# The ends of two attentions on TensorE: output products cut into parts, and the orders at the two layer borders changed

## What is computed

```
for l in range(2):
    proj = h @ w_in[l]            # a, g, zc, q, k, v, za, qi, ki, wi
    y_conv = silu(layer_norm(conv31(a * sigmoid(g)))) * silu(zc)
    y_attn = topk_masked_attention(q, k, v, qi, ki, wi) * silu(za)
    h = layer_norm(ALPHA * h + concat(y_conv, y_attn) @ w_out[l])
x = h[16:528]
z = rmsnorm(x) @ w_in_2           # q, k, v, gate_a, u, v_in, gate_b, g_merge
attn = softmax(q k^T) v * silu(gate_a)
gm = gelu(u) * mix(layernorm(gelu(v_in))) * silu(gate_b)
x = x + (g0 * (attn @ w_proj_attn) + g1 * (gm @ w_proj_gmlp)) @ w_out_2
out = rmsnorm(x)
```

## Time and profile before

| | |
|---|---|
| median of 3 runs | 1014.51 us (1014.0 to 1015.2) |
| the profiled execution | 1014.03 us, span 1012.2 us |
| mean granted clock of TensorE | 0.991 |
| TensorE busy | 982.5 us (97%) |
| VectorE busy | 668.4 us (66%) |
| ScalarE busy | 559.6 us (55%) |
| GpSimd busy | 232.4 us (23%) |
| chain that ended last | TensorE 80%, VectorE 10%, ScalarE 3%, DMA 2% |

### The profile page before, as it was taken

One profiled execution on the slowest core, in us unless ns is written; L12 is line 12 of the kernel. 1 busy time (PEld: TensorE's weight loads), 2 busy tenths in 40 slices (PEclk: granted clock), 3 DMA queues, 4 the chain that ended last, 5 costly groups with the idle time before them and its releaser, 6 DMA issues.

```text
span 1012.2 us, 15815 instructions
## 1 busy us (share of the span) xinstructions
PE 982.5 (97%) x6084; PEld 819.3 (81%) x6084; DVE 668.4 (66%) x1444; ACT 559.6 (55%) x920; POOL 232.4 (23%) x254
## 2 busy tenths in 40 slices
PE   8999999999999999999999999999999999999997
PEld 7888998986677988888878677888888788888886
DVE  4899999988673499999988756638522333333432
ACT  6685891655343568598165424544646566564442
POOL 0110671125212401077111511624101000000001
PEclk9999999999999999999999899999999999999999
DMA  8876885752001577487475300478777536366662
GB/s 299 198 183 169 214 195 135 174 118 85 1 1 66 143 186 175 121 192 183 125 170 122 118 21 1 169 172 199 180 215 198 116 87 162 88 162 129 173 160 83
DMA packets 23962, 143.92 MB, mean 142 GB/s; under 512 B 2880, under 2 KB 3648, under 8 KB 8272
## 3 DMA queue, kind: packets, MB, share of 16 engines
q0 software_dynamic: 8496, 60.36, 32.2%
q1 hardware_dynamic: 15392, 82.55, 23.0%
HBM read 140.81 MB, written 2.10 MB: 141 GB/s over the span
## 4 chain that ended last, share of the span: by engine, by line
PE 80%; DVE 10%; ACT 3%; issue 2%; POOL 2%; DMA 2%; SPq 1%; POOLq 0%; DVEq 0%; ACTq 0%
PE psum_B L1404 20%; PE psum_A L1404 13%; PE psum_B L1438 8%; PE psum_A L1438 8%; PE psum_A L1600 6%; DVE conv_acc L1918 4%; PE psum_C L1480 2%; PE psum_C L1404 2%; PE psum_A L1815 2%; PE psum_B L1815 2%; DMA w_raw<-in_weights 2%; PE psum_B L1544 2%; POOL w_lo L1184 2%; PE psum_B L1802 2%; PE psum_A L1516 2%
## 5 line engine op out<-in xcount | busy, mean ns | idle before, releaser
L1191 POOL DMA_DIRECT2D w_lo<-in_weights x59 | 52.0, 881 | 545.9 <-ACT w_lo L728 493.7
L1918 DVE SCALAR_TENSOR_TENSOR conv_acc<-u,vec,conv_acc 128x528 f32<-128x528 f32 (+1 forms) x240 | 172.4, 756 | 3.2
L1404 PE MATMUL psum_B<-x_hi,w_hi 128*128 128x272 f32 (+3 forms) x456 | 138.1, 337 | 0.5 <-ACT shifted L785 0.3
L1404 PE MATMUL psum_B<-x_hi,w_lo 128*128 128x272 f32 (+3 forms) x456 | 135.4, 331 | 0.0
L1404 PE MATMUL psum_B<-x_lo,w_hi 128*128 128x272 f32 (+3 forms) x456 | 135.3, 331 | 0.0
L727 ACT ACTIVATE w_hi<-w_raw 128x2048 fp32r<-128x2048 f32 (+2 forms) x73 | 113.4, 1553 | 25.8 <-DMA w_raw<-in_weights 25.3
L728 ACT ACTIVATE w_lo<-w_raw 128x2048 fp32r<-128x2048 f32 (+2 forms) x73 | 112.7, 1545 | 0.0
L1404 PE MATMUL psum_A<-x_hi,w_hi 128*128 128x272 f32 (+3 forms) x368 | 100.1, 315 | 0.8 <-DMA w_lo<-in_weights 0.4
L1404 PE MATMUL psum_A<-x_lo,w_hi 128*128 128x272 f32 (+3 forms) x368 | 98.1, 309 | 0.0
L1404 PE MATMUL psum_A<-x_hi,w_lo 128*128 128x272 f32 (+3 forms) x368 | 97.9, 309 | 0.0
L1404 PEld LDWEIGHTS psum_B<-x_hi,w_hi 128*128 128x128 f32 (+1 forms) x456 | 79.0, 187 | 10.0 <-issue 1.7
(11 more groups left out here) (409 smaller groups left out, 2294.9 us busy)
## 6 DMA issues: line engine op xcount, KB each, us to landing
w_raw<-in_weights SPq DMA_DIRECT2D x65, 1024.0 KB, 5.0
w_lo<-in_weights POOLq DMA_DIRECT2D x57, 1024.0 KB, 8.3
x_first<-in_x_t SPq DMA_DIRECT2D x8, 264.0 KB, 6.3
h<-in_x SPq DMA_DIRECT2D x1, 2048.0 KB, 9.8
out<-h SPq DMA_DIRECT2D x4, 512.0 KB, 2.6
w_raw<-in_weights SPq DMA_DIRECT2D x2, 512.0 KB, 7.6
post_ln_g<-in_post_ln_g SPq DMA_DIRECT2D x2, 512.0 KB, 4.6
post_ln_b<-in_post_ln_b SPq DMA_DIRECT2D x2, 512.0 KB, 6.3
```

What stands on the lines that cost most here:

```text
L1191: pool.dma_start(wlo[n % RING][:, 0:width], io["weights"][n, :, 0:width], accum_op=ALU.add) \
L1404: mm = pe.matmul(ps[0:cols, i, o:o + b - a], w[wp][:, kt, at:at + cols], x[xp][:, kt, a:b], start=(kt == 0 and wp + xp == 0), stop=(kt == ...
L1918: got = dve.scalar_tensor_tensor(dst, src, w, dst, ALU.mult, ALU.add)
```

## The change

The tables that hang work on the items change. In the first layer the last product of tile 3 (half 1) is cut in two: the convolution's part of tile 4 runs behind item 36, tile 3's first part behind item 37 and its second behind item 38, in bank 1 of `psum_C`. In the second layer the two parts of tile 3 stand behind items 28 and 29, and the convolution's part of tile 4 is cut into six products behind item 30 and six behind item 31. In the first layer the normalisation of tile 3 moves behind the loop, tile 3 is turned behind both attention parts, and the second half of GpSimd's second subtraction waits for tile 4's normalisation. Behind the second layer both `h_normed` buffers lie in `k`, the first two are written ahead of the gated output, ScalarE takes `x_hi` of tile 1 ahead of the weights, and `kv` of t = 3 stands two query products later, with tile 4 turned behind the first query product.

```
-        (34, 0, 3, "A"), (36, 1, 3, "A")),
-    1: ((17, 0, 1, "A"), (19, 0, 2, "B"), (21, 1, 1, "A"), (23, 1, 2, "A"), (26, 0, 3, "A"), (28, 1, 3, "A")),
+        (34, 0, 3, "A")),
+    1: ((17, 0, 1, "A"), (19, 0, 2, "B"), (21, 1, 1, "A"), (23, 1, 2, "A"), (26, 0, 3, "A")),
...
-OUTPUT_CONV_AT = {0: 38, 1: 30}
+LAST_OUTPUT_AT = {
+    0: ((36, "wo conv", 0, 0, 4), (37, "wo part", 0, 1, 3, "C", 0, 4), (38, "wo part", 1, 1, 3, "C", 0, 4)),
+    1: ((28, "wo part", 0, 1, 3, "A", 0, 4), (29, "wo part", 1, 1, 3, "A", 0, 4), (30, "wo conv", 0, 0, 2),
+        (31, "wo conv", 0, 2, 4)),
+}
...
-KV_AND_Q = (("kv", 0), ("kv", 1), ("kv", 2), ("q", 0, 0), ("kv", 3), ("q", 1, 0), ("q", 2, 0), ("q", 3, 0),
+KV_AND_Q = (("kv", 0), ("kv", 1), ("kv", 2), ("q", 0, 0), ("q", 1, 0), ("q", 2, 0), ("kv", 3), ("q", 3, 0),
...
-        hn = [sb("h_normed0", [P, D], at=K_AT + 4 * D), sb("h_normed1", [P, D], at=where[0])]
+        hn = [sb(f"h_normed{i}", [P, D], at=K_AT + 4 * D * i) for i in range(2)]
...
                 y_hi(l, "attn", 4)
+                if l == DEPTH - 1:
+                    x_hi(l, 1)
                 split_hi(after)
...
-                subtract_hi(after + 1)
-                ln_deviation((l, "post", 4), 4, P)
+                if l < DEPTH - 1:
+                    subtract_hi(after + 1, (0,))
+                    ln_deviation((l, "post", 4), 4, P)
+                    pool.wait_ge(normed.sem, normed.at((l, "x", 4)))
+                    subtract_hi(after + 1, (1,))
...
-                    if t == 2:
-                        turn_rows(1, 4)
                 else:
                     query_half(t, *half)
+                    if (t, *half) == (0, 0):
+                        turn_rows(1, 4)
```

More of the change, by code:

```diff
@@ L346, in attention_extras @@
         todo["dve"][i + 1].append(("residual", part, t))
+    todo["dve"][39 if l == 0 else 29].append(("residual", 1, 3))
     for t, i in POST_AT[l]:
@@ L353, in attention_extras @@
             todo["pool"][i + 1].append(("input", t))
-    todo["pe"][OUTPUT_CONV_AT[l]].append(("wo conv", 0))
+    for i, *op in LAST_OUTPUT_AT[l]:
+        todo["pe"][i].append(tuple(op))
+    if l == 0:
+        todo["dve"][39].append(("aggregate", 3))
+        todo["pool"][39].append(("deviation", "post", 3))
     if l == 0:
@@ L1585, in turn_rows, with output_half @@
                 mm.then_inc(psum_full.mark(use), 1)
-            def output_half(l, n, half, t, ps):
+            def output_half(l, n, half, t, ps, kks=range(4)):
                 part = ("conv", "attn")[half]
@@ L1593, in output_half @@
                     pe.wait_ge(meta_paired.sem, meta_paired.at((l, part)))
-                for kk in range(4):
+                for kk in kks:
                     kt = half * 4 + kk
@@ L1608, in output_rows, with output_part, output_conv @@
                 output_half(l, n, 1, t, ps).then_inc(psum_full.mark(use), 1)
-            def output_conv(l, n):
+            def output_part(l, half, n, t, buf, first, last):
+                use = (l, "wo", n, t)
+                ps = (bank[buf][:, 1:2, :] if half else claim(use, buf, (1,)))[:, 0, :]
+                mm = output_half(l, n, half, t, ps, range(first, last))
+                if half and last == 4:
+                    mm.then_inc(psum_full.mark(use), 1)
+            def output_conv(l, n, first=0, last=4):
                 buf, at = OUTPUT_BANK[n]
-                ps = claim((l, "wo", n, 4), buf, (at,))[:, 0, :]
-                output_half(l, n, 0, 4, ps).then_inc(psum_full.mark((l, "wo", n, 4, "conv")), 1)
+                ps = (bank[buf][:, at:at + 1, :] if first else claim((l, "wo", n, 4), buf, (at,)))[:, 0, :]
+                mm = output_half(l, n, 0, 4, ps, range(first, last))
+                if last == 4:
+                    mm.then_inc(psum_full.mark((l, "wo", n, 4, "conv")), 1)
             def output_attn(l, n):
@@ L1707, in woven @@
                             output_rows(l, *op[1:])
+                        elif op[0] == "wo part":
+                            output_part(l, *op[1:])
                         else:
@@ L1733, in _ @@
                     turn_rows(l, 2)
+                    output_attn(l, 1)
                 turn_rows(l, 3)
-                output_attn(l, 1)
+                if l == DEPTH - 1:
+                    output_attn(l, 1)
             SPARE = "B", (1,)
@@ L2125, in aggregate, with post_norm @@
                     .then_inc(stats_made.mark((l, "post", t)), 1)
-            def post_norm(l, t):
+            def post_norm(l, t, between=None):
                 n = SIZE[t]
@@ L2135, in post_norm @@
                     .then_inc(dve_step.mark((l, "gain", t)), 1)
+                if between:
+                    between()
                 dve.wait_ge(dve_step.sem, dve_step.at((l, "gain", t)))
@@ L2237, in _ @@
                     woven(i + 1)
-                y_part(l, "attn", 4)
                 if l < DEPTH - 1:
+                    post_norm(l, 3, lambda: y_part(l, "attn", 4))
                     x_lo(l, 0)
                     x_lo(l, 1)
+                    residual(l, 0, 4)
+                    x_lo(l, 2)
+                    residual(l, 1, 4)
+                    aggregate(l, 4)
+                    post_norm(l, 4)
+                    x_lo(l, 3)
                 else:
@@ L2245, in _ @@
                     second_input(2)
+                    y_part(l, "attn", 4)
+                    second_input(3)
                     x_lo(l, 1)
-                    second_input(3)
                     x_lo(l, 2)
[L2249 to L2256, removed]
+                    residual(l, 0, 4)
+                    x_lo(l, 3)
+                    residual(l, 1, 4)
+                    aggregate(l, 4)
+                    post_norm(l, 4)
                     second_input(4)
```

6 lines of the change are left out of this document (4 added, 2 removed).

## The result

The changed kernel takes 1017.64 us (median of 20 runs) where the kernel before takes 1013.73 (20 runs): a ratio of 1.0034, 95% interval 1.0023 to 1.0044, so 2.3 to 4.5 us slower. Two of the changed kernel's runs took 1199 and 1363 us at granted clocks of 0.75 and 0.66, and one of the kernel before 1082; the ratio leaves these three out (without them the medians are 1017.5 and 1013.6). The forecast was 1018.0 in a range of 1013.0 to 1021.5, and slower by over 0.2% with a chance of 0.60.

The account below looks back on a forecast made before the run. TensorE, busy 97% of the span, bounds the kernel. Minus 1.2 (first layer), plus 2.95 (late `vin` half 1), plus 1.7 (clock) is plus 3.45 on 1014.03: 1017.5, with 0.5 for the median 1018.0 us, range 1013.0 to 1021.5.

Parts of the forecast that it names:

- The step that decided: First product with `vin` half 1: the block lands at 691.6, TensorE stands 5.6 us, and the product starts 2.95 us later.
- Rival A: At `vin` half 1: the block arrives in time and the change does what it removes, 1010.6 us; chance 0.14.
- rival B: At `vin` half 1: TensorE stands, but at the short end of both transfers, 1015.9 us; chance 0.13.
- The chain: From `kv` of t = 3 to `vin` half 1: issue 0.2, load 8.1, copies and issue 4.1, adding DMA 9.6 us.
- The guess that the loads of `u` slow the adding DMA: At `vin` half 1: two `u` loads follow its adding DMA, taken at 9.6 us, bounds 8.1 and 10.8.
- The second layer's gain: Second layer's tail and border up to the queries: four waits of 3.10 us go, two cuts cost 0.4, minus 2.7 us.
- rival D: First query product: held up to 0.9 us by the copy of `kv` of t = 0; slower still, 1022.0 us; chance 0.10.
- The first layer's gain: First layer's tail: waits of 0.82 and 0.69 us go, 0.2 and 0.1 are added, minus 1.2 us.
- The 0.1 us for the second half of the last subtraction: First layer: GpSimd's second subtraction half starts only when tile 4 is normalised; product g may wait, 0.1 us taken.
- The clock: Behind the stand at `vin` half 1: TensorE's clock falls and costs 1.7 us, bounds 0 and 3.3.
- Rival C: At `vin` half 1: TensorE stands 5.6 us and the clock holds, 1016.3 us; chance 0.08.
- the forecast's sentence that two loads cost more than one: Adding DMA of `vin` half 1: two loads behind it cost it more than one does; no run showed two.

Follow-up runs that it names:

- experiment 1: Changed kernel, but `kv` of t = 3 stands one query product later than in the kernel before, not two: 1013.99 us, ratio 1.000.
- experiment 2: Kernel before with only the change's order of `kv` and `q` and tile 4 turned behind the first query product: 1022.52 us, ratio 1.0086.
- experiment 3: Changed kernel with `kv` of t = 3 and the turn of tile 4 at the places of the kernel before: 1011.84 us, ratio 0.998.
- experiment 7: Changed kernel, but GpSimd makes the low part of `vin` half 1 by subtractions, not an adding DMA: 1012.23 us, ratio 0.9979.
- experiment 6: Changed kernel, but the loads of both `u` blocks are issued only when the first `vin` product has ended: 1024.3 us, one run.
- experiment 4: Changed kernel with all edits to the second layer's end and the border behind it undone, only the first layer's part left: 1011.89 us, ratio 0.9979.
- experiment 5: Changed kernel with 24 products whose result nothing reads, between half 0 and half 1 of the first `vin` product: 1015.58 us, ratio 1.0014.
- second trace: Changed kernel run again unedited for another trace: 1019.5 us against 1014.9, ratio 1.0049; the traced execution took 1017.55 us.
- experiment 8: Changed kernel with `kv` of t = 3 one query product later than before and `vin` half 1 subtracted by GpSimd: 1009.0 us, ratio 0.9956; repeated, 1009.1.
- experiment 9: As experiment 8, but ScalarE copies `u` half 1 right behind `u` half 0 and its adding DMA is issued there: 1010.31 us, ratio 0.9965.
- experiment 10: As experiment 8, but ScalarE copies `kv` of t = 0 out of its bank ahead of the squares of tile 4: 1008.8 us, ratio 0.9943.

## Why the prediction was right

**The step that decided held.** The forecast had TensorE stand 5.6 us at the first product with `vin` half 1; it stood 5.86 and 5.10. (Counted as the forecast counts, from start to start, with six blocks of 2.725 us, these are 6.6 and 5.5.) Experiments 1, 2, 3 and 7 tell it from the rivals: the stand shrinks by a block when `kv` goes one block back, comes alone with that order in the kernel before, and goes with the order undone or the chain shortened. Rival A (the block arrives in time) is refuted, and so are the short transfers of rival B: the chain took 21.9 us or more in the traces of the changed kernel and of experiment 2, where B has 20.0.

**The chain, term by term.** Issue 0.2 us, as estimated. Load 8.6 and 8.3 for 8.1. Copies and issue 4.08 for 4.1. Adding DMA 10.0 and 9.2 for 9.6. In all 22.98 for 22.0 in the first trace, 21.87 in the second (667.93 to 689.80). The guess that the loads of `u` slow the adding DMA is shown by experiment 6. One reading was not exact: the adding DMA of 680.20 was said to run alone for its 8.1 us, but the loads of `u` were issued at 686.15, 2.2 us before it landed. Really alone it took 8.2 (experiment 6), so nothing hung on it. The rates of a transfer beside another were taken from neighbours in the trace of before, and that was good to half a microsecond.

**The second layer's gain** was put at 2.7 and is 2.6: ScalarE's copy at 571.67 stood at 572.65, so the trace was 0.98 late there; 664.03 and 5.45 and 0.98 is 670.46, and `kv` of t = 3 started at 667.87. The 0.48 for the copy of `kv` of t = 0, counted at nothing with a bound of 0.9, is in it: the mechanism that rival D named was real, at half its price. GpSimd's subtractions fell from 3.2 to 3.4 us to 2.40 to 2.44, as the change means them to; I had them cancel against ScalarE's order, and no wait on them came up.

**The first layer's gain** was put at 1.2. The traces have 1.41, 1.39 and 1.35 between the copies at 246 and 349, and the runs of experiment 4 have 2.1 (1.3 to 2.9). The 0.1 us for the second half of the last subtraction did not show.

**The clock** was put at 1.7 us lost, bounds 0 and 3.3. It cost 2.55 and 2.1 in the two traces, 1.65 in experiment 2, and 2.1 by the runs of experiment 5. The term was somewhat small for this kernel. It had been taken from the kernel's first products, which follow 4.61 us without work, and from two falls in the attention (1.8, 1.5 and 3.3 us lost). The 6.8 us of low clock of rival D came too (692.2 to 699.0 in the first trace), but 1.5 us of them fell into the stand, and 2.5 in the second trace. Rival C (the clock holds) is refuted for stands of 3.66 us and more, and holds for 2.82 in one trace: that case I did not have. It fits that experiment 1 equals the kernel before, give or take 1 us, where one with the lower clock would be some 2 us slower.

**The sum.** The three terms, by the trace: the first layer minus 1.4 in both; where `vin` half 1 starts, against the kernel before and less what the trace was already behind or ahead at the turn of 619.88, plus 4.0 in the first (5.04 less 1.01) and plus 2.9 in the second (1.12 and 1.79), for 2.95; the clock plus 2.55 and plus 2.1, for 1.7. That is plus 5.2 and plus 3.6. The forecast was 3.45, and the runs say 3.4 (by the ratio) to 3.9 (by the medians). So each term was right to half a microsecond in the second trace. In the first the chain and the clock took 1.1 and 0.4 us more, and both traces are of the same kernel: that the median came out within 0.4 us of the forecast is partly luck. Why the transfers took 1.1 us more in one execution than in the other stays open; in the first the loads of `u` followed the adding DMA sooner (0.9 us, not 1.2).

The profile of before had no wait on the block that decided. It showed instead a transfer with 0.4 us to spare at the end of 21.4, and a table that says which product frees its slot.

## What to carry to other kernels

Before a product is moved, ask whose slot it frees: a weight ring ties the load of a later block to the last use of an earlier one, and moving a short product by two blocks moved a chain of 22 us that no list of waits named. Where such a chain is too long, it can be shortened at the dearest link (two subtractions of 2.6 us for an adding DMA of 10), but then everything queued behind it on that engine moves too. And a reorder that trades several small waits for one long one loses more than the sum, since behind the long one TensorE's clock was low (here from a stand of 3.66 us on).

## What the runs showed of the hardware

TensorE at 1.00 granted, with full work ahead, and what a stand did to the twelve products behind it (2.73 us in a row without a stand):

| stand, us | experiment | twelve products, us | granted clock |
|---|---|---|---|
| 2.82 | 1 | 2.85 | 1.00 throughout |
| 3.66 | 6, at `u` | 4.24 | 0.50 for 3.0 us of products |
| 4.07 | 6, at `vin` | 5.03 | 0.50 for 4.5 |
| 5.10 | changed kernel, second trace | 4.84 | 0.50 for 4.2 |
| 5.34 | 2 | 4.38 | 0.50 for 3.3 |
| 5.86 | changed kernel, first trace | 5.28 | 0.50 for 5.3 |

The loss, 1.5 to 2.55 us, does not grow with the stand: the low stretch began inside the stand in every case, but only 0.1 us ahead of its end in experiment 2 and 2.5 in the second trace. Filling the stand with useless products kept the clock and gained 2.1 us. The Trainium skill, "TensorE: Matmul & The Clock Gate", section "Why this matters for your kernels", asks that long idle gaps between bursts of products be avoided, since the clock falls back to half in them; the runs agree, with five stands of 3.66 us and more behind which it was low and one of 2.82 behind which it was not.

An adding DMA of 1 MB alone landed in 8.2 us (experiment 6), and the fastest from 655 to 735 us of all traces, with others beside them, in 7.9. The sooner another transfer followed it, the longer it took. With the two plain loads of `u` 6 us behind it, it took 8.1 to 8.3 us in three traces; 3.3 us behind it (experiment 1) 8.7; 1.2 to 0.9 us behind it 9.2 to 10.0. One plain load 0.5 us behind it made it 10.8 to 11.1 in the kernel before and in experiments 3 and 4, and 11.6 to 12.0 in experiments 1, 8, 9 and 10; where that difference comes from was not settled. So the forecast's sentence that two loads cost more than one is neither shown nor refuted: no run has both at the same distance. A second adding DMA 5.4 us behind a first takes 8.4 to 9.6, 3.6 to 4.1 us behind it 10.7 to 11.7.
